# Gate and up of a decoder step: three products split once more, three summed in PSUM, and a weight ring of 256 columns

## The reference, cut to what matters

```python
D_MODEL, D_FF = 1024, 2816
h2 = rmsnorm(x, norm2_g)
x = x + (jax.nn.silu(h2 @ w_gate) * (h2 @ w_up)) @ w_down
y = rmsnorm(x, final_norm_g)
```

## Time and profile before

| | us |
|---|---|
| three runs: lowest, median, highest | 1315.94, 1317.72, 1318.37 |
| profiled execution, span from first to last instruction | 1315.8 |
| TensorE busy with matmuls in it | 1279.8 (97%) |
| VectorE, ScalarE, GpSimd busy | 825.0 (63%), 508.5 (39%), 426.5 (32%) |
| before gate and up starts | 591.7 |
| turn 0 | 49.3 (591.7 to 641.0) |
| turns 1 to 10 | 421.0 (641.0 to 1062.0) |
| down stage and end | 253.8 |

### The profile page before, as it was taken

One profiled execution on the slowest core, in us unless ns is written; L12 is line 12 of the kernel. 1 busy time (PEld: TensorE's weight loads), 2 busy tenths in 40 slices (PEclk: granted clock), 3 DMA queues, 4 the chain that ended last, 5 costly groups with the idle time before them and its releaser, 6 DMA issues.

```text
span 1315.8 us, 23632 instructions
## 1 busy us (share of the span) xinstructions
PE 1279.8 (97%) x9276; PEld 1200.3 (91%) x9276; DVE 825.0 (63%) x1259; ACT 508.5 (39%) x881; POOL 426.5 (32%) x278
## 2 busy tenths in 40 slices
PE   9999999999999989999999999999999999999997
PEld 8788998888786569999999999999999999999987
DVE  5883166776765436279843455444553579899986
ACT  7333234665655342125322222222222234444462
POOL 1642344354431227650334444444444400000000
PEclk9999999999998999999999999999999999999998
DMA  9321102000027535621222112212222288868503
GB/s 330 131 62 33 48 5 75 5 22 1 17 68 273 192 152 177 199 90 34 95 74 90 65 66 89 82 66 72 82 76 88 85 331 274 282 208 271 162 1 136
DMA packets 70377, 151.58 MB, mean 115 GB/s; under 512 B 9138, under 2 KB 16690, under 8 KB 69842
## 3 DMA queue, kind: packets, MB, share of 16 engines
q1 hardware_dynamic: 70290, 150.39, 34.0%
HBM read 127.80 MB, written 22.56 MB: 114 GB/s over the span
## 4 chain that ended last, share of the span: by engine, by line
PE 78%; DVE 10%; issue 4%; ACT 3%; DMA 2%; SPq 1%; POOL 1%; DVEq 0%; POOLq 0%; ACTq 0%
PE ps L1012 23%; PE ps L1014 23%; PE ps L1013 23%; PE ps L1241 2%; DMA araw<-in_w_dn 1%; PE ps L1299 1%; PE ps L1253 1%; DVE hL L2199 1%; PE ps L1361 1%; PE ps L1254 1%; SPq L571 1%; DVE nmx L2394 1%; ACT pTH L1636 1%; PE ps L1326 1%; DVE prob L2388 1%
## 5 line engine op out<-in xcount | busy, mean ns | idle before, releaser
L981 POOL TENSOR_TENSOR ws<-wraw,ws 128x1024 fp32r<-128x1024 f32 x50 | 124.5, 2490 | 214.0 <-ACT ws L1636 214.0
L1012 PE MATMUL ps<-bHL,aHL 128*128 128x272 f32 x616 | 178.2, 289 | 3.7 <-DVE bHL L2843 3.6
L1014 PE MATMUL ps<-bHL,aHL 128*128 128x272 f32 x616 | 177.2, 288 | 0.0
L1013 PE MATMUL ps<-bHL,aHL 128*128 128x272 f32 x616 | 177.1, 288 | 0.0
L2686 DVE TENSOR_TENSOR bufP<-bufP,ps 128x544 f32<-128x544 f32 x66 | 47.5, 721 | 134.3 <-PE ps L1014 132.0
L1636 ACT ACTIVATE ws<-wraw 128x1024 fp32r<-128x1024 f32 x55 | 58.4, 1061 | 172.6 <-PE ps L1014 168.8
L1012 PEld LDWEIGHTS ps<-bHL,aHL 128*128 128x128 f32 x616 | 116.0, 188 | 4.6 <-DVE bHL L2843 4.6
L1013 PEld LDWEIGHTS ps<-bHL,aHL 128*128 128x128 f32 x616 | 116.0, 188 | 0.0
L1014 PEld LDWEIGHTS ps<-bHL,aHL 128*128 128x128 f32 x616 | 115.9, 188 | 0.0
L1004 POOL TENSOR_TENSOR rt<-ms,mhalf 128x3 f32<-128x3 f32 (+1 forms) x3 | 4.4, 1463 | 249.5 <-DVE ms L2877 249.5
L1636 ACT ACTIVATE aHL<-araw 128x512 fp32r<-128x512 f32 x66 | 41.8, 633 | 92.7 <-DVE araw L2815 45.7
(11 more groups left out here) (379 smaller groups left out, 4438.1 us busy)
## 6 DMA issues: line engine op xcount, KB each, us to landing
araw<-in_w_dn SPq DMA_DIRECT2D x121, 256.0 KB, 3.5
wraw<-in_w_gu SPq DMA_DIRECT2D x44, 512.0 KB, 3.5
cp<-in_cache SPq DMA_DIRECT2D x64, 272.0 KB, 4.6
ab<-acts SPq DMA_DIRECT2D x34, 272.0 KB, 4.2
raw<-in_w_out SPq DMA_DIRECT2D x16, 512.0 KB, 4.1
acts<-bufC SPq DMA_DIRECT2D x22, 272.0 KB, 2.1
xt<-in_x_tok SPq DMA_DIRECT2D x9, 512.0 KB, 6.8
x<-x2s SPq DMA_DIRECT2D x8, 544.0 KB, 5.8
```

The source lines that it names most:

```text
L981: pool.tensor_tensor(w[:, 1, :], w_source(j), w[:, 0, :], ALU.subtract).then_inc(cw_lo, 1)
L1012: nc.tensor.matmul(out, wh, xh, start=start, stop=False)
L1013: nc.tensor.matmul(out, wh, xl, start=False, stop=False)
L1014: return nc.tensor.matmul(out, wl, xh, start=False, stop=stop)
```

## The change

Only gate and up change, and what follows of it for buffers at the start of the down stage.

- **Ring.** The weight passes in chunks of 256 columns: a ring of 10 chunks of 128x256 (high and low), in the place of two pieces. A product is four whole steps (g, kh) of 12 matmuls, each with its own chunk.
- **Second level.** P4 and P3 from turn 2 on, and P2 from turn 3 on, are split by the same seven-product scheme once more: seven sub-steps of 6 matmuls, each with a chunk. The sub-products 1, 6, 7 and 4 follow each other in one PSUM bank, 5 and 3 in a second, 2 has a third. VectorE takes each sub-step's sum out with an operation of 128x272. Each split product needs four sums of 256 weight columns per turn, and three factors of the input and one changed quarter, made once, in turns 1 and 2 (for P2 its input block is first put together again by GpSimd).
- **PSUM.** P1, P6 and P7 follow each other in the same banks without a new start, and ScalarE copies the bank after each of them to bufC, bufP and bufD (`copy_chain`); VectorE then adds P2, P5 (twice), P4 and P3. The order within a turn is new (`turn_steps`).
- **Unrolled.** The loops over turns are gone: each engine runs through one list of steps (`PLAN`), and copies, Silus and sums have fixed places in it.
- **Down stage.** The buffers bHL, bsum, ab2, ab3 and sqh are moved, and the first loads and steps wait for other counts.

The new functions are cut here to what sets order and waits:

```diff
+SPLIT_FROM = {"P4": 2, "P3": 2, "P2": 3}
+def turn_steps(i):
+    middle = parts("P6", (1, 0))
+    if split(i, "P2"):
+        a, b, c, e = middle
+        middle = [("P2", 1), ("P2", 2), a, ("P2", 6), ("P2", 5), b, ("P2", 7), c, ("P2", 3), e, ("P2", 4)]
+    else:
+        middle = parts("P2", (1, 0)) + middle
+    end = parts("P4", (1, 0)) + parts("P3", (0, 1))
+    if split(i, "P4"):
+        end = [("P4", 1), ("P4", 2), ("P3", 1), ("P3", 5), ("P4", 6), ("P4", 5), ("P3", 6), ("P3", 2),
+               ("P4", 7), ("P4", 3), ("P3", 7), ("P3", 3), ("P4", 4), ("P3", 4)]
+    return parts("P1", (1, 0)) + middle + parts("P7", (1, 0)) + parts("P5", (0, 1)) + end
 # SP
+            def turn(i, last=False):
...
+                sp_.wait_ge(blocks, 4 * i + 1)
+                store_act(i, 0, bufC[:, 1, :])
                 if last:
                     load_ab0(0, TURNS - 1)
 # GpSimd
+            def chunk_low(n):
+                i, step = PLAN[n]
+                pool.wait_ge(cw_hi, PROD + n + 1)
+                x = chunks[n % CHUNKS]
+                pool.tensor_tensor(x[:, 1, :], source_of(i, step), x[:, 0, :], ALU.subtract).then_inc(cw_lo, 1)
+            for n, (i, step) in enumerate(PLAN):
+                chunk_low(n)
+                if (i, step) == (2, ("P7", 0, 1)):
+                    factor_back()
 # TensorE
+            def sub_step(n, i, p, q):
+                b = PRODUCT_BANK[p] + SUB_BANK[q]
+                if q in (6, 7, 4, 3):
+                    pe.wait_ge(added, taken(i, p, {6: 1, 7: 6, 4: 7, 3: 5}[q]))
...
+                elif p == "P3":
+                    pe.wait_ge(added, taken(i, "C22", 1 if q == 2 else 0))
...
+                for k in range(2):
+                    at = slice(P * k, P * k + P)
+                    ins = mm3(ps[:, b, 0:SUB], w[:, 0, at], w[:, 1, at], *factor_of(i, (p, q), 0, k),
+                              q in (1, 2, 5) and k == 0, k == 1, q in (6, 7, 4, 3))
+                ins.then_inc(prod, 1)
 # whole_step: before P6, P7 and P4 a wait for copy_chain of P1, P6 and P7 of the same g
 # ScalarE
+            def chunk_high(n):
...
+                    act.wait_ge(prod, 2 * PROD + n - CHUNKS + 1)
+                act.wait_ge(*source_ready(i, step))
+                hi(chunks[n % CHUNKS][:, 0, :], source_of(i, step)).then_inc(cw_hi, 1)
+            for n, (i, step) in enumerate(PLAN):
+                at_end = step == turn_steps(i)[-1]
+                if step[0] in ("P1", "P6", "P7") and step[2] == 1:
+                    copy_chain(i, step[0], step[1])
+                if step == ("P7", 1, 1):
+                    silu_of(i, bufC, *(("P2", 3) if split(i, "P2") else ("P2", 0)))
+                elif step == ("P5", 1, 0):
+                    silu_of(i, bufC, "C22", 0)
...
+                if n + CHUNKS < len(PLAN):
+                    chunk_high(n + CHUNKS)
...
+                if at_end:
+                    silu_of(i, bufD, *(("P4", 3) if split(i, "P4") else ("P4", 0)))
+                    silu_of(i, bufP, *(("P3", 3) if split(i, "P3") else ("P3", 0)))
 # VectorE
+            def take_fifth(i, g):
...
+                nc.vector.tensor_tensor(x, x, pair(4 + 2 * g), ALU.add).then_inc(added, 1)
+                dve.wait_ge(kept, copied(i, "P7", g))
+                dve.wait_ge(act_out[0], 16 * i + 16)
+                nc.vector.tensor_tensor(halves(bufC[:, g, :]), halves(bufD[:, g, :]), pair(4 + 2 * g), ...
+            for i, step in PLAN:
+                if step == ("P1", 1, 0):
+                    weight_sum(i, "S1")
+                    weight_sum(i, "S2")
+                    if split(i, "P2"):
+                        sub_sums(i, "P2")
+                    weight_sum(i, "S3")
+                    if i == 1:
+                        factor_sums("P4")
+                        factor_sums("P3")
+                    else:
+                        gated_block(i - 1, 3, bufD, ...)
+                        gated_block(i - 1, 4, bufP, ...)
+                elif step == ("P7", 1, 0):
+                    weight_sum(i, "S4")
+                    if split(i, "P4"):
+                        sub_sums(i, "P4")
+                        sub_sums(i, "P3")
+                elif step == ("P7", 0, 0):
+                    gated_block(i, 1, bufC, ...)
...
+                elif step == ("P5", 0, 0) and i == 2:
+                    factor_sums("P2")
...
+                elif step[0] == "P5" and step[2] == 1:
+                    take_fifth(i, step[1])
+                elif len(step) == 2:
+                    take_sub(i, *step)
+                if step == ("P5", 1, 1):
+                    gated_block(i, 2, bufC, "C22", 1)
...
+                elif i == 2 and step == ("P3", 2):
+                    factor_low("P2", (1, 2, 4, 3), 8)
+                if i == TURNS - 1 and step == ("P4", 7):
+                    down_low(0)
```

More of the change, by code:

```diff
@@ L117, in xt_rows, with split, parts, done @@
     return min(P, T - XT_AT[b])
+def split(i, p):
+    return p in SPLIT_FROM and i >= SPLIT_FROM[p]
+def parts(p, gs):
+    return [(p, g, kh) for g in gs for kh in range(2)]
+def turn_steps(i):
[10 more added lines that the diff above has]
+    return parts("P1", (1, 0)) + middle + parts("P7", (1, 0)) + parts("P5", (0, 1)) + end
+PLAN = [(i, step) for i in range(1, TURNS) for step in turn_steps(i)]
+PLACE = {event: n for n, event in enumerate(PLAN)}
+def done(i, *step):
+    return 2 * PROD + PLACE[i, step] + 1
+def all_done(i, p):
+    return 2 * PROD + max(n for (j, step), n in PLACE.items() if j == i and step[0] == p) + 1
+def all_low(i, p):
+    return all_done(i, p) - PROD
+ALL_DONE, ALL_LOW = 2 * PROD + len(PLAN), PROD + len(PLAN)
+def sum_names(i):
+    subs = {p: [f"{p}s{x}" for x in (1, 3, 2, 4)] if split(i, p) else [] for p in ("P2", "P4", "P3")}
+    return ["S1", "S2", *subs["P2"], "S3", "S4", *subs["P4"], *subs["P3"]]
+SUM_AT = {event: 4 + n + 1 for n, event in enumerate((i, s) for i in range(1, TURNS) for s in sum_names(i))}
+def taken_by(step):
+    if len(step) == 2:
+        return [step]
+    p, g, kh = step
+    if kh == 0 or p in ("P1", "P6", "P7"):
+        return []
+    return [("C12", g), ("C22", g)] if p == "P5" else [(p, g)]
+TAKEN = {event: SUMS + n + 1 for n, event in enumerate((i, e) for i, step in PLAN for e in taken_by(step))}
+def taken(i, *event):
+    return TAKEN[i, event]
+def copied(i, p, g):
+    return 2 + 6 * (i - 1) + 2 * ("P1", "P6", "P7").index(p) + 2 - g
 def xt_of(t):
@@ L749, in load_down @@
                     sp_.dma_start(araw[:, SLOTS[t % RING], 1, :], d["w_dn"][3, k, :, :]).then_inc(ff_full[SLOTS[t % RING]], 16)
[L751 to L756, removed]
+            turn0()
+            for i in range(1, TURNS):
+                turn(i, last=i == TURNS - 1)
             rows_back = {(1, 2, 5, 7)[m % KH] if m >= KH else 2 * (m % KH) + 1 + 2 * TURNS: m for m in range(KD)}
@@ L1009, in _, with mm3 @@
         def _(pe):
[L1010 to L1014, removed]
+            def mm3(out, wh, wl, xh, xl, start, stop, onto=False):
+                nc.tensor.matmul(out, wh, xh, start=start, stop=False, skip_group_check=onto)
+                nc.tensor.matmul(out, wh, xl, start=False, stop=False, skip_group_check=onto)
+                return nc.tensor.matmul(out, wl, xh, start=False, stop=stop, skip_group_check=onto)
             def sum_squares(j, bank, sq, k, n):
@@ L1597, in _ @@
                 w, x = weights_of(t), bHL[t % RING]
-                for o in range(KH):
+                order = (1, 0, 3, 2) if t == 0 else range(KH)
+                for o in order:
                     if p == M7 + 1 and k == 0:
@@ L2099, in turn @@
                     down_high(0)
                     act_high(0)
+                elif i == TURNS - 1 and step == ("P3", 2):
                     down_high(1)
-                silu(i, bufC[:, 0, :], 11)
-                if not last:
-                    weights_high(i + 1, 0, 1 - par)
-                silu(i, bufP[:, 0, :], 13)
-            with act.Fori(0, (TURNS - 3) // 2) as i:
-                for r in range(2):
-                    turn(2 * i + (1 + r), 1 - r)
-            turn(TURNS - 2, 1)
```

448 lines of the change are left out of this document (342 added, 106 removed).

## The result

The changed kernel takes 1319.3 us against 1317.5 of the kernel before run beside it: a ratio of 1.0017, 95% interval [1.0009, 1.0024]. The forecast was 1312. Nothing was gained, though the 156 matmuls are gone from the trace (9120 instead of 9276). The profiled span is 1318.1 us, 2.3 longer than before.

The account below looks back on a forecast made before the run. TensorE's matmuls were taken to bound gate and up. 19.5 us saved, less 3.6 (front), 2.5 (turn 1), 5 (turn 2) and 2.5 (end), left 5.9 off the 1315.8 span: 1309.9, as a median 1312, range 1302 to 1322.

Parts of the forecast that it names:

- What bounds it, and what is removed: Gate and up: TensorE's matmuls bound each turn; 26 split products, 6 matmuls fewer each, save 19.5 us.
- The front: Start of a split turn: P6 waits 0.35 us for ScalarE's P1 copy, P2.6 0.1; 3.6 us over 8 turns.
- The upper bound of 1.65: Most that the front of a split turn was to lose, in us, said to come from rival (d).
- rival (d): GpSimd and VectorE's shared port becomes the bound; a turn takes about 41.9 us, the kernel 1325; chance 0.15.
- The back: Late in a split turn: P4.1 is taken at 32.65 us, TensorE wants P4.6 at 32.75; costed at nothing.
- Rival (c): Block 0's store lands 0.8 us later each turn, so P4.6 waits 0.8; no gain left, 1318 us; chance 0.2.
- Turns 1 and 2: Making the factors delays chunks, copies and takes: 2.5 us lost in turn 1, 5 in turn 2.
- The end: Last turn: the activations' load waits for block 0's store, delaying P3.4 and the down stage; 2.5 us lost.
- The three signs that were named for the forecast: TensorE idle some 0.4 us before P6, 2 to 3.6 in turn 1, and the largest hole in turn 2.

Follow-up runs that it names:

- e9: Changed kernel with ScalarE's P1 copies ahead of the Silus, and C22's gate behind the takes of P4.1 and P4.2; median 2 us under its expected 1309 to 1311.
- e12: e11 with 10 ring chunks again and VectorE's turn 1 sums of factors ahead of S3; 1300.7 us, 1.2% faster than the kernel before.
- e2: Changed kernel with P2 never split, P4 and P3 still split; its ten turns take 414.0 us against 424.1.
- e5: Changed kernel with C22's gate behind the takes of P4.1 and P4.2 instead of ahead; median 0.2 us above its expected 1314 to 1316.
- e7: Changed kernel with P2 split from turn 4 and its factors made in turn 3; turn 2 takes 41.04 us, turn 3 43.81.
- e11: e8 with GpSimd's four sums for P2's factors spread over four chunks of turn 2; turn 3 takes 40.69 us, turn 2 40.70.
- e8: Changed kernel with P1 copies before Silus, C22's gate later, P2's factors in turn 3, 8-chunk ring; missed its expected 1300 to 1304 by 1.5 us.
- e6: Changed kernel with a first ring of 8 chunks and the last turn's first two down-stage steps 10 sub-steps later; turn 1 takes 42.29 us.

## Why the prediction was wrong

- **What bounds it, and what is removed: right.** In e9 turns 3 to 9 take what their matmuls take. No run gets all of the 19.5 us; in e12, with 25 split products instead of 26, the ten turns take 404.7 us, 16.3 less than before, of 18.8 that its matmuls make.
- **The front: order right, size too small.** In turn 7 the copy of P1 ran from 7.24 to 7.84 (forecast 7.14 to 7.76), 0.3 after TensorE's 7.52. But that is a good turn. In turns 4 to 10 the place costs 0.52 to 1.26, and in turn 3 nothing: 0.64 in the mean of the eight turns, where 0.35 was forecast. In turn 5, for one, S2 and the first sum of P2 both meet a chunk. Each hole is also followed by a gap of 0.20, 0.075 over the pace, which the sum didn't have. Before P2.6 it cost 0.19 in place of 0.1. Together 0.83 for 0.45: 6.6 us for the term of 3.6. The upper bound of 1.65 doesn't follow from rival (d) as the prediction says: that rival's turn of 41.9 is 2.05 over 39.85.
- **The back: "It fits with 0.1 us, so I cost it at nothing" is the step that failed.** The term put at nothing measured 2.8 us in turns 3 to 10, 0.35 a turn (0.15 to 0.55), and 1.3 more in turn 2. In turn 7 the take of P4.1 ended at 33.2 (32.74 and 0.44), forecast 32.65: the second half of C22 ended at 31.6 instead of 31.3, since it follows a take that waits for TensorE and not for the store, and its gate took 1.12 and ended at 32.8 instead of 32.3. TensorE, itself late from the front, could have begun P4.6 at 33.06 and did at 33.32. In e2, where no hole stands in front, the place costs the same 0.33 in every turn. Rival (c) named this very place, though its cause, a late store, wasn't there: C22's first half began at 28.2, before the 29.05 of the sum. e5 removes the hole by order alone.
- **Turns 1 and 2: mechanism right, size off by 1.8 and 2.9.** In turn 1 the hole cost 2.6 with the gap behind it, forecast 2.5; the rest, 1.6, is nearly all low clock, which the forecast didn't have. In turn 2 the holes before P3.1, before P4.6 and behind the late take of P4.7 are those that were named; they cost 3.0, 1.3 and 2.8 in place of 5 in all, and low clock adds 0.8, and 0.75 in turn 3. The low clock was bad luck in part: the same hole of turn 1 had none behind it in e2 and e7.
- **The end: wrong in sign.** The load of the activations went at 26.9 us into the last turn and its first use began at 37.2 (forecast 29.2 and 39), so the hole of 2.5 us wasn't there. The store of block 0 lands nearly 1 us sooner than the sum had it (28.2 for 29.05 in turn 7), and in the last turn the load goes 2.3 sooner. The down stage and the end took 252.2, 1.6 less than before; in the twelve other kernels they take 251.8 to 254.0, so the 1.6 tells little.
- **The port, rival (d): not the bound.** GpSimd was busy 29.9 of 40.87 us in turn 7, as forecast (30), is named in none of TensorE's waits in the changed kernel, and e9 keeps the collisions without a hole. The rule of the Trainium skill (SBUF — State Buffer, "SBUF: two separate sides") is that a VectorE operation with two SBUF inputs and a GpSimd operation exclude each other for a whole instruction. The gates of 1.07 to 1.24 us against 0.72 agree with it. It is no bound for a turn here, as the instructions that wait are not those that TensorE waits for, once the order is right.

In all, the steady turns took 6.7 us more than forecast (8 x 0.84: 0.38 in front, 0.35 in the back, 0.09 of low clock in turn 3, the rest in spacing), turn 2 2.9, turn 1 1.8, the start of turn 1 0.8, and the end 4.1 less: 8.1, against the 8.2 between a span of 1309.9 and the 1318.1 measured. Without the error at the end, which ran the other way by luck, the miss would have been 12.3. The three signs that were named for the forecast (ScalarE's copy before P6, turn 1's hole, turn 2's largest hole released by VectorE) all came; they show the mechanism and not its size.

## What to carry to other kernels

When a bound engine gets shorter steps, list for each of its waits what stands ahead of the releaser in that engine's queue: here a Silu, a gate and a sum, none of them urgent, held back what 26 split products saved. Moving them and the factors, with one split less, gave 18.6 us (1319.3 to 1300.7). A chain that fits by a tenth of a microsecond is to be priced at the spread of its durations between turns (here 0.15 to 0.55 us late), not at nothing. One-time work, here the factors, was free when it was spread (e11), and dear where three engines handed it on in one piece (turn 2 of the changed kernel, turn 3 of e8).

## What the runs showed of the hardware

TensorE's granted clock fell to 0.5 (1.2 GHz) behind 9 of the 19 holes of 2.2 to 3.04 us in gate and up (the changed kernel, e2 to e7 and e9), and behind none of up to 1.64. The length doesn't decide alone: 2.67 was followed by it (e6), 2.73 (e6) and 3.04 (the changed kernel) were not, and the hole of 2.61 to 2.64 in turn 1, the same in seven of these kernels, was followed by it in five. Where the clock fell, it cost 1.5 to 1.6 us. At full clock the holes of every length seen, short ones too, are followed by one matmul distance of 0.20 us (0.23 at most) instead of 0.125.
